# Odd layer of a two-layer backbone: one convolution beside the head projections, the normalised layer input kept in memory, and a reciprocal in four pieces

## The chip, the cores and the metric

The kernel runs on one core of a Trainium2 chip. The metric is the device time of one execution in microseconds (us), from the first to the last instruction of the core with what lies around it. TensorE is called PE in the rows, VectorE DVE, ScalarE ACT, GpSimd POOL, and SyncE SP (it only issues transfers here). A name with q behind it (SPq, ACTq) is the part of an engine that issues transfers.

## The reference, cut to what matters

The stream has 1024 latent tokens (a grid 64 wide) and 256 context tokens, 1024 wide: 10 tiles of 128 tokens, 8 latent (`LT`) and 2 context (`NT` = 10). Two layers are computed. Even layer: attention of 8 heads with 2 key heads, beside a gated product. Odd layer, at the core of this case:

```
h = rms_norm(x, norm1_g) * (1 + scale) + shift        # per stream
p = h @ w_in                                           # 1024 -> 2560 columns
q, k = per-head rms_norm of p[:, 0:512], p[:, 512:1024];  v = p[:, 1024:1536]
neighbourhood attention(q, k, v, bias tables from rpb) # latent tokens; keys also of the context
y = p[:, 1536:2048] * sigmoid(p[:, 2048:2560])         # latent tokens
y = conv(y, dw, 31 taps along the tokens, each of 512 channels by itself) + dw_b
d = silu(layer_norm(y))                                # over the 512 channels
x = x + gate * (concat(attention, d) @ w_out)
```

Each layer ends with a mixture of 16 experts (top 2 within one group of four). All arithmetic is fp32. Where the kernel can, it splits an operand into a rounded part (`hi`, type fp32r) and the rest (`lo`) and forms a product as three fast ones: hi·hi, hi·lo, lo·hi.

## The kernel before, in words

The program is a list of stages (`Phase`), each with its own buffers and semaphores, and a barrier of all engines at its end; within a stage each engine has its own list of instructions, written by hand, and waits on semaphores. `build` calls them in order: modulation, `project_even`, `attend_even`, experts and `combine` of layer 0, `project_conv` (its tiles carry the prefix pc_), `project_odd` (po_), attention of the odd layer (at_), `output_odd`, experts and `combine` of layer 1. The weights for `project_conv` (cw_w) are loaded and split during `combine`.

**The layer input.** `NormStage` makes the normalised, modulated and transposed input of one tile: load x (L277), sum of squares on ACT (L293), mean on DVE (L300), power on POOL (L307, `rstd`), scale on DVE (`scale`, L312), eight transposes on PE (L322), modulation on DVE from PSUM (`modulate`, L333, eight instructions), rounding on ACT (`round_hi`, L341), rest on POOL (`rest_lo`, L345). The product is then 24 matmuls for each 512 output columns (`product`, L354). Both `project_conv` (latent tiles) and `project_odd` (all ten) run it, so eight tiles are normalised twice.

**`project_conv`.** For each latent tile: products g and a (48 matmuls), sigmoid on ACT (L767), y on DVE (L903), four transposes of y on PE (`transpose_y`, L931), copy into yT on ACT (L769). POOL also multiplies 31 taps into diagonal matrices for two of the four channel blocks (L841), and after the tiles makes the bias rows of the attention in 16 pieces of 8 columns (L818), which it stores to memory. Then the convolution of 1024 tokens in two halves q of 512: channel blocks 0 and 1 on PE, 31 matmuls each with the diagonals (L964); blocks 2 and 3 on DVE, one instruction for each tap (`convolve`, L865; the first tap L861), two blocks in turn. Then for each half mean (PE, L953), subtraction (`centre`, DVE, L872), square (ACT, L789), variance (PE, L953), root (ACT, L783), reciprocal (L879) and multiplication (L882) on DVE, silu (ACT, L794), and a store.

**`project_odd`.** It loads and splits three 512-column parts of w_in in 16 pieces (L391, L398, L405), then for each tile: products q, k and v (72 matmuls; 48 for context tiles), squares on ACT (L1064, L1066), sums on DVE (L1127, L1129), the power -1/2 on POOL (L1099), multiplications on DVE from PSUM (L1137, L1138: `qk_done`), head gains on POOL for q (L1103) and on DVE for k (L1141), transposes (L1160, L1167), split on ACT and DVE (L1072, L1076, L1144, L1148), and stores from the ACT queue. PE starts the q product of the next tile when `qk_done` has come. SP also copies the bias rows into 96 tables, memory to memory (L1028).

**`attend_even`** runs by a planner: `EvenPlan` writes one list of events for all engines; `finish` and `prepare` give each event of a tile a due place from 0 to 19 among the tile's score steps. The event `normal` holds the reciprocal of the softmax sums (L1523, 512 columns) and the multiplication behind it (L1527); 'max' events (L1510) on DVE free the PSUM banks into which PE writes the next scores (L1599) and transposes (L1635).

Of the kernel before, what the change touches and what calls it, by code (L numbers as in the profile page):

```python
# [31 lines left out]
P = 128  # L32
D = 1024
KD = D // P
# [659 lines left out]
def project_conv(nc, k, w, dw, dw_b, ln_g, ln_b, rpbs, skews):  # L694

    CC = BW // P
    QT = 4 * P
    PC = 2  # L700
    NQ = SEQ // QT
    with Phase(nc, "pc") as ph:
        tiles = list(range(LT))
        ns = NormStage(ph, k, 1, tiles, k.stream_mid, False)
        sg, y = ph.sb("sg", [P, BW]), ph.sb("y", [P, BW])
        yT = ph.sb("yT", [P, CC, SEQ + 2 * HALO])
        acc = [ph.sb(f"acc{q}", [P, CC, QT]) for q in range(NQ)]
        diag = [ph.sb(f"diag{c}", [P, CONV, P]) for c in range(PC)]
        eps = ph.sb("eps", [P, 1])
        sq = ph.sb("sq", [P, CC, QT])  # L710
        rstd = ph.sb("rstd_c", [P, QT])
        var = ph.sb("var", [P, QT])
# [15 lines left out]
        DVE_CHUNKS = list(range(PC, CC))  # L728
        ND = len(DVE_CHUNKS)

        with nc.Block() as block:

            @block.sync
            def _(sp):
                ns.load_columns(sp)
                ns.load(sp, 0)
                ns.load(sp, 1)
                sp.wait_ge(R["zero"], 2)
                for o in range(2):
                    sp.dma_start(bias_rows[o][:, P // 2 - 16:P // 2 + 15], rpbs[o].rearrange("h r c -> (h r) c")).then_inc(R["bias_in"], 16)  # L740
                for i in range(2, LT):
                    ns.load(sp, i)
# [7 lines left out]
            def _(act):  # L750
# [2200 lines left out]
```

## Time and profile before

| what | value |
|---|---|
| median of 3 runs | 3231.34 us (3231.14 to 3236.19) |
| the profiled execution, its own time | 3228.54 us |
| its span | 3226.8 us |
| PE busy | 2489.5 us (77%) |
| DVE busy | 1559.2 us (48%) |
| ACT busy | 1006.9 us (31%) |
| POOL busy | 605.6 us (19%) |
| granted clock of PE, mean | 0.887 of full speed |

The table gives shares of the whole span. The kernel is a row of stages with different limits, so a share says little about one of them; the rows below are of the stages that the change touches. The chain that ended last reaches back only to 3164 us, within the last stage, so it doesn't help here.

### The profile page before, as it was taken

The page shows a single profiled execution, that of the slowest core. Times are in us where ns is not written, and L with a number is a line of the kernel's source. Part 1 is how long each engine was busy: PE and PEld are TensorE (multiplying, and loading weights), DVE is VectorE, ACT ScalarE, POOL GpSimd, SP SyncE. Part 2 cuts the span into 40 slices and gives each one's busy share as a digit, 9 for nine tenths or more (in the row PEclk, how much of TensorE's full clock was granted, in tenths as well). Part 3 has the DMA queues.
Part 4 walks back from the last instruction along what each step waited for, and adds up shares of the span by engine and source line. Part 5 has one row for each costly group of instructions (what it writes and reads, how often), then busy time and mean ns, then how long its engine had stood idle before and what let it go on. Part 6 is the DMA issues. An engine that isn't in the chain of part 4 may idle for free. (4 is left out here: it accounts for less than half of the span.)

```text
span 3226.8 us, 31983 instructions
## 1 busy us (share of the span) xinstructions
PE 2489.5 (77%) x10785; PEld 1803.0 (56%) x10786; DVE 1559.2 (48%) x2144; ACT 1006.9 (31%) x1326; POOL 605.6 (19%) x560
## 2 busy tenths in 40 slices
PE   5499788898943999999217778498699773999990
PEld 0388655565622888887005533376465662888770
DVE  2255553443333566555442494333477225566754
ACT  1122143233312455444001101222265112455640
POOL 0233212111112000000122340133131332000002
PEclk9999899998966999999558889699899885999995
DMA  9210236111046767663860140665683325778846
GB/s 388 64 50 36 89 131 221 42 47 59 30 178 164 290 253 272 228 248 118 340 234 27 55 135 13 164 154 135 182 214 87 125 90 200 270 271 307 322 176 221
DMA packets 304557, 534.58 MB, mean 166 GB/s; under 512 B 126157, under 2 KB 150203, under 8 KB 298300
## 3 DMA queue, kind: packets, MB, share of 16 engines
q1 hardware_dynamic: 228848, 387.56, 35.9%
q0 software_dynamic: 25520, 85.58, 7.7%
q10 hardware_dynamic: 50076, 59.99, 5.4%
q8 instruction: 64, 1.05, 0.1%
q14 instruction: 49, 0.40, 0.0%
HBM read 431.72 MB, written 116.03 MB: 170 GB/s over the span
## 5 line engine op out<-in xcount | busy, mean ns | idle before, releaser
L2597 DVE TENSOR_TENSOR ex_gu_lo<-mw_gu,ex_gu_hi 128x2048 fp32r<-128x2048 f32 x128 | 287.4, 2288 | 77.8 <-ACT ex_gu_hi L2517 77.5
L2517 ACT ACTIVATE ex_gu_hi<-mw_gu 128x2048 fp32r<-128x2048 f32 x128 | 237.5, 1910 | 122.9 <-DVE ex_y L2644 117.6
L1627 PE MATMUL at_ps_o<-at_pT,at_v_one 128*128 128x512 f32 x336 | 177.6, 610 | 12.5 <-ACT at_total L1409 9.4
L2675 PE MATMUL ex_ps_g<-ex_gu_hi,ex_xT_hi 128*128 128x512 f32 x408 | 169.1, 414 | 8.7 <-issue 5.3
L2675 PE MATMUL ex_ps_y<-ex_d_hi,ex_hT_hi 128*128 128x512 f32 x408 | 166.5, 408 | 9.1 <-DVE ex_d_lo L2597 7.7
L2597 DVE TENSOR_TENSOR ex_d_lo<-mw_d,ex_d_hi 128x2048 fp32r<-128x2048 f32 x64 | 143.8, 2288 | 53.3 <-ACT ex_d_hi L2517 53.3
L2492 POOL TENSOR_TENSOR ex_at<-ex_slots,ex_nil 128x1 int32<-128x1 int32 x53 | 17.7, 333 | 801.2 <-PE ex_ps_x L2669 796.6
L2675 PE MATMUL ex_ps_g<-ex_gu_lo,ex_xT_hi 128*128 128x512 f32 x408 | 164.1, 402 | 0.0
L2675 PE MATMUL ex_ps_g<-ex_gu_hi,ex_xT_lo 128*128 128x512 f32 x408 | 164.0, 402 | 0.0
L1399 ACT ACTIVATE at_pT<-at_ps_s 128x512 f32<-128x512 f32 x168 | 99.0, 595 | 204.6 <-PE at_ps_s L1620 204.2
L2675 PE MATMUL ex_ps_y<-ex_d_lo,ex_hT_hi 128*128 128x512 f32 x408 | 161.7, 396 | 0.0
L2675 PE MATMUL ex_ps_y<-ex_d_hi,ex_hT_lo 128*128 128x512 f32 x408 | 161.7, 396 | 0.0
L2675 PE MATMUL ex_ps_u<-ex_gu_hi,ex_xT_hi 128*128 128x512 f32 x408 | 161.2, 395 | 0.0
L2675 PE MATMUL ex_ps_u<-ex_gu_lo,ex_xT_hi 128*128 128x512 f32 x408 | 161.2, 395 | 0.0
L2675 PE MATMUL ex_ps_u<-ex_gu_hi,ex_xT_lo 128*128 128x512 f32 x408 | 161.1, 395 | 0.0
L2517 ACT ACTIVATE ex_d_hi<-mw_d 128x2048 fp32r<-128x2048 f32 x64 | 119.1, 1909 | 29.4 <-DVE ex_y L2619 20.7
L1510 DVE TENSOR_REDUCE at_mx<-at_ps_t 128x1 f32<-128x512 f32 (+1 forms) x168 | 108.6, 683 | 25.6 <-PE at_ps_t L1599 25.1
L2006 PE MATMUL at_ps_o<-at_pT,at_vo 128*128 128x512 f32 (+3 forms) x256 | 113.2, 523 | 1.2 <-ACT at_pT L1829 0.8
L865 DVE SCALAR_TENSOR_TENSOR pc_acc<-pc_yT,pc_taps,pc_acc 128x512 f32<-128x512 f32 x120 | 112.9, 1017 | 0.0
L964 PE MATMUL pc_ps_c<-pc_yT,pc_diag 128*128 128x512 f32 x248 | 109.9, 604 | 1.6 <-ACT pc_acc L776 1.6
L1599 PE MATMUL at_ps_t<-k_both,at_q_both 128*128 128x512 f32 (+1 forms) x208 | 99.4, 546 | 14.7 <-DVE at_mx L1510 10.9
L2517 ACT ACTIVATE ex_xT_hi<-ex_ps_x 128x512 fp32r<-128x512 f32 x106 | 57.8, 596 | 169.2 <-PE ex_ps_x L2669 169.2
(492 smaller groups left out, 5907.1 us busy)
## 6 DMA issues: line engine op xcount, KB each, us to landing
mw_gu<-in_moe_w_gate SPq DMA_DIRECT2D x32, 2048.0 KB, 10.7
mw_gu<-in_moe_w_up SPq DMA_DIRECT2D x32, 2048.0 KB, 15.7
mw_d<-in_moe_w_down SPq DMA_DIRECT2D x32, 2048.0 KB
y_d<-ex_y ACTq DMA_DIRECT2D x51, 512.0 KB
mod_mod_w<-in_ada_w SPq DMA_DIRECT2D x24, 1024.0 KB, 10.9
y_d<-at_zero POOLq DMA_DIRECT2D x36, 512.0 KB, 5.1
co_mod_w<-in_ada_w SPq DMA_DIRECT2D x16, 1024.0 KB, 13.8
edge_d<-rows_d SPq DMA_DIRECT2D x64, 160.0 KB, 3.4
```

The source lines that it names most:

```text
L865: ins = nc.vector.scalar_tensor_tensor(acc[q][:, c, :], src, taps[:, c, t:t + 1], acc[q][:, c, :], ALU.mult, ALU.add)
L964: mm = nc.tensor.matmul(ps_c[:, :], diag[c][:, t, :], yT[:, c, q * QT + t:q * QT + t + QT], start=(t == 0), stop=(t == CONV - 1))
L1399: nc.scalar.activation(pT[u % 3][:, :], ps_s[u % 3][:, :], ACT.Exp).then_inc(S["exp_done"], 1)
L1510: nc.vector.tensor_reduce(mx[:, heads[0]:heads[-1] + 1, c], src.rearrange("p (h t) -> p h t", t=size), AX.X, ALU.max).then_inc(read, 1)
L1599: mm = nc.tensor.matmul(flat[:, n * size:(n + 1) * size], q_both[i % 2][g][:, j * P:(j + 1) * P], k.k0_both[:, g, a:a + size], start=True, ...
L1627: nc.tensor.matmul(ps_o[:, :], v_one[:, kt, g:g + 2, :].rearrange("p a d -> p (a d)"), pT[u % 3][:, :], start=(u == plan.first[i, g]), sto ...
L2006: nc.tensor.matmul(ps_o[g][:, c0 * P:c1 * P], vo[h % 2][:, kt, :, :].rearrange("p a d -> p (a d)"), pT[s % 3][:, 0:n], start=(s == plan.fi ...
L2492: nc.gpsimd.tensor_tensor(at[:, :], slots[:, bass.ds(within(n, most), 1)], nil[:, :], ALU.add).then_inc(S["at_ready"], 1)
L2517: nc.scalar.activation(dst, src, ACT.Copy).then_inc(sem, 1)
L2597: sub = lambda dst, a, b, sem: nc.vector.tensor_tensor(dst, a, as_f32(b), ALU.subtract).then_inc(sem, 1)
L2675: mm = nc.tensor.matmul(out, a[:, c, :], b[:, c, cols], start=(c == 0 and j == 0), stop=(c == chunks - 1 and j == 2))
```

## The change

It does three things.

1. `project_conv` and `project_odd` are replaced by `project_tiles` and `project_heads`, with `OddShared` holding what both need. `project_tiles` normalises all ten tiles once and stores the hi and lo parts of each to a new memory tensor hT_d; makes a, g and y of the latent tiles as before; loads and splits the q and k weights between the tiles (two pieces of 512 columns each tile); makes the bias rows between the tiles, in 32 pieces of 4 columns; and starts the first 48 table copies from tile 5 on. No convolution is in it.
2. `project_heads` loads the hi and lo parts from memory instead of normalising, splits the v weights on ACT and POOL, and computes the heads as before with single instead of double output buffers and the stores moved to SP. The convolution of all four channel blocks runs on DVE between the head instructions: 124 instructions, each over all 1024 tokens of a block. Mean, variance and what follows them stand among the two context tiles. The diagonal matrices and their matmuls are gone.
3. In `attend_even` the reciprocal is cut in four of 128 columns, at due places 1, 1, 2 and 3, and what follows it is due one place later.

Core of the diff:

```diff
@@ project_tiles
-        tiles = list(range(LT))
-        ns = NormStage(ph, k, 1, tiles, k.stream_mid, False)
+        tiles = list(range(NT))
+        ns = NormStage(ph, k, 1, tiles, k.stream_mid, True)
...
-                ns.load_columns(sp)
                 ns.load(sp, 0)
                 ns.load(sp, 1)
+                ns.load_columns(sp)
...
+                for i in range(NT):
+                    if i + 2 < NT:
+                        ns.load(sp, i + 2)
+                    sp.wait_ge(ns.lo_done, i + 1)
+                    for n, src in enumerate((ns.hi, ns.lo)):
+                        sp.dma_start(k.hT_d[i, n], as_f32(src[i % 2][:, :, :])).then_inc(h_out[i % 2], 16)
+                    if i + 1 < LT:
+                        o.w_qk.load(sp, 2 * i + 2, 2 * i + 4)
...
+                    if i >= 5:
+                        o.copy_tables(sp, k, 0, 10 * (i - 5), 10 * (i - 4))
...
                     if i < LT:
+                        o.w_qk.round_hi(act, 2 * i, 2 * i + 2)
+                    if 0 < i <= LT:
                         j = i - 1
                         act.wait_ge(S["gemm_g"], i)
...
+                    if i == 0:
+                        pool.wait_ge(R["bias_in"], 32)
+                    if i < LT:
+                        for n in range(NP * i // 4, NP * (i + 1) // 4):
+                            mask_rows(n)
...
+                    if i < LT:
+                        o.w_qk.rest_lo(dve, 2 * i, 2 * i + 2)
@@ project_heads
+        wv_hi, wv_lo, wv_raw = w.hi[:, :, 0:BW], w.lo[:, :, 0:BW], w.raw
...
+        acc = ph.alias("acc", w.lo, [P, KD, 2 * BW])[:, :, BW:2 * BW]
...
+                for c in range(KD):
+                    pool.wait_ge(S["wv_hi"], c + 1)
+                    nc.gpsimd.tensor_tensor(wv_lo[:, c, :], wv_raw[c % 2][:, :], as_f32(wv_hi[:, c, :]), ALU.subtract).then_inc(S["wv_lo"], 1)
...
+                def convolve(n):
+
+                    for t, c in steps[done[0]:done[0] + n]:
+                        src = o.yT[:, c, t:t + SEQ].rearrange("p (q t) -> p q t", q=NQ)
...
+                            dve.wait_ge(S["conv_done"], done[0] - CC + 1)
+                            ins = nc.vector.scalar_tensor_tensor(both(c), src, o.taps[:, c, t:t + 1], both(c), ALU.mult, ALU.add)
...
                 dve.wait_ge(S["gains_in"], 32)
...
+                convolve(8)
+                for j in range(NT):
...
+                    convolve(5)
...
+                    nc.vector.tensor_reduce(stat[:, h0:], per_head(sq[:, c0:]), AX.X, ALU.add).then_inc(S["sums_done"], 1)
...
+                    convolve(4)
...
+                    convolve(6)
+                    dve.wait_ge(S["kT_hi"], j + 1)
...
+                    product(ps_k[:, :], j, o.w_qk.hi, o.w_qk.lo, BW).then_inc(S["gemm_k"], 1)
+                    if j == LT:
+                        mean(0)
+                        mean(1)
+                    if j == LT + 1:
+                        variance(0)
@@ EvenPlan.finish
-        return [(1, ('normal', i)), (3, ('mixed', i)), (5, ('out', i, 0)), (8, ('out', i, 1)), (11, ('square', i)), (12, ('mean', i)),
...
+        return [(1, ('invert', i, 0)), (1, ('invert', i, 1)), (2, ('invert', i, 2)), (3, ('invert', i, 3)), (3, ('normal', i)),
+                (4, ('mixed', i)), (6, ('out', i, 0)), (9, ('out', i, 1)), (12, ('square', i)), (13, ('mean', i)),
```

Names as in the rows: cv_ is what `OddShared` holds (yT, taps, the q and k weights), po_acc the sum of the convolution.

VectorE, one latent tile of the head stage. Before (with the normalisation of the next tile in it):

```order
L333 TENSOR_SCALAR po_hf<-po_pt,po_cols 128x128 x8
L300 TENSOR_SCALAR po_ms<-po_ss 128x1
L312 TENSOR_SCALAR po_x<-po_x,po_rstd 128x1024
L1127 TENSOR_REDUCE po_stat<-po_sq 128x16
L1129 TENSOR_SCALAR po_stat<-po_stat 128x16
L1137 TENSOR_TENSOR po_qk<-po_ps_q,po_r 128x512
L1138 TENSOR_TENSOR po_qk<-po_ps_k,po_r 128x512
L1141 TENSOR_TENSOR po_qk<-po_qk,po_gains 128x512
L1144 TENSOR_TENSOR po_k_lo<-po_ps_kT,po_k_hi 128x512
L1148 SCALAR_TENSOR_TENSOR po_q_lo<-po_ps_qT,po_q_hi 128x512
```

and now:

```order
L1076 SCALAR_TENSOR_TENSOR po_acc<-cv_yT,cv_taps,po_acc 128x2x512 x5
L1102 TENSOR_REDUCE po_stat<-po_sq 128x16
L1104 TENSOR_SCALAR po_stat<-po_stat 128x16
L1076 SCALAR_TENSOR_TENSOR po_acc<-cv_yT,cv_taps,po_acc 128x2x512 x4
L1117 TENSOR_TENSOR po_qk<-po_ps_q,po_r 128x512
L1118 TENSOR_TENSOR po_qk<-po_ps_k,po_r 128x512
L1120 TENSOR_TENSOR po_qk<-po_qk,po_gains 128x512
L1076 SCALAR_TENSOR_TENSOR po_acc<-cv_yT,cv_taps,po_acc 128x2x512 x6
L1128 TENSOR_TENSOR po_k_lo<-po_ps_kT,po_k_hi 128x512
L1132 SCALAR_TENSOR_TENSOR po_q_lo<-po_ps_qT,po_q_hi 128x512
```

The ten instructions of the normalisation have left the stage; 15 of the convolution stand in their place, nine of them ahead of `qk_done` (L1118).

VectorE in `attend_even`, where the sums of one tile are inverted while the maxima of the next are taken. Before:

```order
L1501 SCALAR_TENSOR_TENSOR at_q_rest<-at_ps_t,at_q_both 64x512 x2
L1523 RECIPROCAL at_sums<-at_sums 128x512
L1527 TENSOR_TENSOR at_aT<-at_total,at_sums 128x512
L1510 TENSOR_REDUCE at_mx<-at_ps_t 128x1 x3
L1531 TENSOR_TENSOR at_aT_lo<-at_ps_t,at_aT_hi 128x512
```

and now:

```order
L1508 SCALAR_TENSOR_TENSOR at_q_rest<-at_ps_t,at_q_both 64x512 x2
L1531 RECIPROCAL at_sums<-at_sums 128x128 x2
L1517 TENSOR_REDUCE at_mx<-at_ps_t 128x1 x2
L1531 RECIPROCAL at_sums<-at_sums 128x128
L1517 TENSOR_REDUCE at_mx<-at_ps_t 128x1
L1531 RECIPROCAL at_sums<-at_sums 128x128
L1536 TENSOR_TENSOR at_aT<-at_total,at_sums 128x512
```

The first maxima stand behind two short reciprocals instead of a long one and the multiplication.

## Rows read from the trace of the kernel before

**Rows 1.** Windows: stretch, length, busy us (count) of PE, PEld, DVE, ACT, POOL, clock, DMA, GB/s.

```profile
1663.00:1851.00 188.00, 119.18 (x484) 96.42 (x485) 59.49 (x104) 25.65 (x40) 52.82 (x38) 0.79 0.17 45
1851.00:2022.00 171.00, 129.11 (x282) 55.03 (x280) 114.58 (x117) 19.53 (x21) 43.11 (x34) 0.88 0.28 81
2022.00:2080.00 58.00, 27.02 (x80) 19.20 (x80) 19.96 (x31) 16.52 (x21) 3.42 (x3) 0.66 0.54 143
2080.00:2287.00 207.00, 168.35 (x745) 135.16 (x745) 72.66 (x154) 42.44 (x71) 66.43 (x35) 0.92 0.57 146
```

**Rows 2.** Timeline, tiles of project_conv: start us, us, instruction, idle before it and releaser.

```profile
1689.98 7.30 DVE L312 TENSOR_SCALAR pc_x<-pc_x,pc_rstd 128x1024 f32<-128x1024 f32 x1 [1.74 <-POOL pc_rstd L307]
...
1747.29 0.60 ACT L769 ACTIVATE pc_yT<-pc_ps_yT 128x512 f32<-128x512 f32 x1 [17.16 <-PE pc_ps_yT L931]
1751.80 0.75 DVE L312 TENSOR_SCALAR pc_x<-pc_x,pc_rstd 128x1024 f32<-128x1024 f32 x1 [0.72 <-POOL pc_rstd L307]
1752.60 1.97 PE L322 MATMUL pc_pt<-ident,pc_x 128*128 128x128 f32 x8 [5.35 <-DVE pc_x L312]
1767.63 0.60 ACT L769 ACTIVATE pc_yT<-pc_ps_yT 128x512 f32<-128x512 f32 x1 [17.28 <-PE pc_ps_yT L931]
```

**Rows 3.** Timeline of the convolution on VectorE, with and without GpSimd at work.

```profile
1904.26 4.82 DVE L865 SCALAR_TENSOR_TENSOR pc_acc<-pc_yT,pc_taps,pc_acc 128x512 f32<-128x512 f32 x4
1905.63 2.90 POOL L818 TENSOR_TENSOR pc_rows<-pc_skew,pc_bias_rows 120x1024 f32<-120x1024 f32 x1 [1.01 <-DMA pc_skew<-in_k_skew]
...
1943.36 2.29 DVE L882 TENSOR_TENSOR pc_acc<-pc_acc,pc_rstd_c 128x2048 f32<-128x2048 f32 x1
1945.57 21.29 DVE L865 SCALAR_TENSOR_TENSOR pc_acc<-pc_yT,pc_taps,pc_acc 128x512 f32<-128x512 f32 x32
```

**Rows 4.** Groups by line in project_conv: busy us, mean ns, idle before.

```profile
L964 PE MATMUL pc_ps_c<-pc_yT,pc_diag 128*128 128x512 f32 x248 | 109.9, 604 | 1.6 <-ACT pc_acc L776 1.6
L818 POOL TENSOR_TENSOR pc_rows<-pc_skew,pc_bias_rows 120x1024 f32<-120x1024 f32 x16 | 41.5, 2594 | 14.3 <-DMA pc_skew<-in_k_skew 14.3
L953 PE MATMUL pc_ps_mu<-pc_acc,pc_mean_w 128*128 128x512 f32 x16 | 7.3, 601 | 1.7 <-DVE pc_acc L865 0.9 <-issue 0.8
```

**Rows 5.** Timeline of one latent tile of project_odd.

```profile
2102.98 0.47 PE L354 MATMUL po_ps_k<-po_w_hi,po_hi 128*128 128x512 f32 x1
2108.68 0.39 PE L354 MATMUL po_ps_v<-po_w_hi,po_hi 128*128 128x512 f32 x1
2111.20 1.21 DVE L1127 TENSOR_REDUCE po_stat<-po_sq 128x16 f32<-128x1024 f32 x1
2112.70 2.91 POOL L1099 TENSOR_TENSOR po_r<-po_stat,mhalf 128x16 f32<-128x16 f32 x1 [2.20 <-DVE po_stat L1129]
2115.65 0.69 DVE L1137 TENSOR_TENSOR po_qk<-po_ps_q,po_r 128x512 f32<-128x512 f32 x1 [3.02 <-POOL po_r L1099]
2117.01 1.79 POOL L1103 TENSOR_TENSOR po_qk<-po_qk,po_gains 128x512 f32<-128x512 f32 x1 [1.40 <-DVE po_qk L1138]
```

**Rows 6.** SP queue in project_odd: the 16 weight pieces.

```profile
2028.07 47.27 SPq L391 DMA_DIRECT2D po_w_raw<-in_od_w_in x16
```

**Rows 7.** Timeline: the last root of project_conv, and the next stage's first instruction.

```profile
2007.75 0.69 ACT L783 ACTIVATE pc_var<-pc_ps_var,pc_eps 128x512 f32<-128x512 f32 x1 [4.19 <-PE pc_ps_var L953]
...
2022.80 2.37 SPq L269 DMA_DIRECT2D po_cols<-mod_d  x4
```

**Rows 8.** The tile edge_d, written by the larger table copies.

```profile
DMA to landing us min/median/max: 2.9/3.6/15.0
```

**Rows 9.** Waits of TensorE in even attention: us in total, times, longest.

```profile
PE at_ps_t L1599 <- DVE at_mx L1510: 10.9, 9, 2.6
PE at_ps_t L1635 <- DVE at_mx L1510: 9.5, 3, 4.1
```

**Rows 10.** The tile at_sums: reciprocals of both sizes, ns min/median/max.

```profile
L1947 DVE RECIPROCAL at_sums<-at_sums x32: 894/940/953, 2351.6 to 2498.8; 128x128 f32<-128x128 f32 x32
L1523 DVE RECIPROCAL at_sums<-at_sums x10: 3333/3334/3353, 452.1 to 896.8; 128x512 f32<-128x512 f32 x10
```

More of the change, by code:

```diff
@@ L1030, in _ @@
[L1030 to L1034 removed]
+                for j in range(NT):
+                    if j + 2 < NT:
+                        load(j + 2)
+                    o.copy_tables(sp, k, 1, 5 * j, 5 * j + 5)
+                    store(j)
+                for q in range(NQ):
+                    sp.wait_ge(S["silu_done"], CC * (q + 1))
+                    sp.dma_start(k.mT_d.rearrange("(c p) t -> p c t", p=P)[:, :, q * QT:(q + 1) * QT], part(q)).then_inc(S["stored"], 16)
@@ L1080, in _, with square, root @@
-                store_heads(NT - 1)
-                for p in range(2):
-                    act.wait_ge(head_out[p], stored(NT - 2 + p))
+                def square(q):
+                    act.wait_ge(S["centred"], q + 1)
+                    if q:
+                        act.wait_ge(S["var_full"], q)
+                    nc.scalar.activation(csq[:, :, :], part(q), ACT.Square).then_inc(S["squared"], 1)
+                def root(q):
+                    act.wait_ge(S["var_full"], q + 1)
+                    nc.scalar.activation(var[:, q, :], var_bank[q][:, 0:QT], ACT.Sqrt, bias=eps[:, 0:1]).then_inc(S["var_ready"], 1)
@@ L1151, in _, with product @@
             @block.tensor
             def _(pe):
-                ns.transposes(pe, 0)
-                def transpose_k(j):
+                def product(out, j, w_hi, w_lo, a, by_chunk=False):
+                    hi, lo = h_hi[j % 2], h_lo[j % 2]
+                    for c in range(KD):
+                        if by_chunk:
+                            pe.wait_ge(S["wv_lo"], c + 1)
+                        for n, (x, y) in enumerate(((hi, w_hi), (hi, w_lo), (lo, w_hi))):
+                            mm = nc.tensor.matmul(out, x[:, c, :], y[:, c, a:a + BW], start=(c == 0 and n == 0), stop=(c == KD - 1 and n == 2))
+                    return mm
@@ L1168, in transpose_k, with mean, variance @@
                         mm.then_inc(S["qT_full"], 1)
+                def mean(q):
+                    pe.wait_ge(S["conv_done"], CONV * CC)
+                    for c in range(CC):
+                        mm = nc.tensor.matmul(mu_bank[q][:, :], mean_w[:, :], acc[:, 2 * c + q, :], start=(c == 0), stop=(c == CC - 1))
+                    mm.then_inc(S["mu_full"], 1)
+                def variance(q):
+                    pe.wait_ge(S["squared"], q + 1)
+                    for c in range(CC):
+                        mm = nc.tensor.matmul(var_bank[q][:, 0:QT], mean_w[:, :], csq[:, c, :], start=(c == 0), stop=(c == CC - 1))
+                    mm.then_inc(S["var_full"], 1)
@@ L1191 @@
+                    product(ps_v[:, :], j, wv_hi, wv_lo, 0, by_chunk=(j == 0)).then_inc(S["gemm_v"], 1)
+                    if j == LT + 1:
+                        variance(1)
+                turn(NT - 1)
 class EvenPlan:
```

544 lines of the change are left out of this document (234 added, 310 removed).

## The prediction

> **What bounds the kernel now.** I read the odd projection first as windows [rows 1]. `project_conv` and `project_odd` take 188 + 171 + 58 + 207 = 624 us of the span of 3226.8. In the first window TensorE is busy 119 of 188 us and VectorE 59: neither is full, so what bounds it is a chain through the engines. The timeline of its tiles [rows 2] shows that chain: the copies of yT stand 1767.63 - 1747.29 = 20.3 us apart, and in each tile TensorE idles 5.35 us until the scaled x comes. The second window is the convolution: 110 us of it are the matmuls with the diagonals [rows 4], and VectorE has 115 busy us beside them, so that the two halves of the work end about together. The third window is 58 us of loading and splitting 16 weight pieces, 47.3 us from first to last issue [rows 6], with TensorE 27 us busy. The fourth is nine tiles in 207 us, TensorE 168 us busy: near its own bound. So the 110 us of convolution on TensorE lie on the path, while VectorE idles 207 - 73 = 134 us in the fourth window. The question is how much VectorE can take there, and what else shares its time.
>
> **VectorE's price for the convolution.** Alone, 32 steps of 512 elements took 21.29 us, 0.665 each; an instruction of 2048 elements took 2.21 us to the start of the next (1945.57 - 1943.36) [rows 3]. A step of 1024 costs between half of 2.21, 1.11, and 0.665 + 512 x (2.21 - 0.665)/1536 = 1.18. I take 1.14, since four blocks in turn leave two more instructions between dependent steps than two did. 124 steps are 141 us.
>
> GpSimd adds to it. In [rows 3] four steps took 4.82 us instead of 4 x 0.665 = 2.66: 2.1 us were lost to one GpSimd instruction of 2.9. In the new head stage GpSimd has two instructions in each tile: the power, 2.91 us with VectorE idle, and the gains of q, 1.79 us, of which some 0.6 were a wait for VectorE's own gains that began together with it, so 1.2 [rows 5]. The power is the unknown: it handles 16 columns only, and no VectorE instruction ran beside it before. Its cost to VectorE lies between 0 and 2.9 us a tile. I take 2.9, since the nearest row, the 2.9 us instruction of [rows 3], held the steps almost whole.
>
> The Trainium skill (SBUF — State Buffer, Who interferes with whom) speaks against this change here: a VectorE instruction with two inputs in SBUF and a GpSimd one that reads SBUF exclude each other for the whole instruction. The trace agrees for the bias rows (2.1 lost of 2.9); for the power no row shows it. By the rule the power costs 2.9 a tile; without it the stage would be 23 us shorter.
>
> **The pace of a head tile.** VectorE does for one latent tile 15 steps (17.1), the sum and its scaling (1.4), two multiplications, the k gains and two splits of 0.6 to 0.7 each (3.3), together 21.8, plus 2.9 and 1.2 for GpSimd, and 0.4 for ScalarE's rounding of q: 26.3 us. TensorE needs three products of 5.7 (2108.68 - 2102.98 [rows 5]), and 1 for transposes, 18 us, 21 with the half clock that it shows after an idle time (eight transposes in 1.97 us at 1752.60 behind 5.35 us idle, granted clock 0.79 in that window) [rows 1, 2]. So VectorE becomes the bound of the latent tiles and TensorE idles 5 to 8 us in each; its slower clock is hidden under VectorE. The normalisation of x is gone from this stage.
>
> **The head stage, summed.** Start: eight v weight pieces, at 47.27/16 = 2.95 us each 24 us; VectorE waits for the gains, which SP issues behind them, although its first steps need no gain. Then 13 steps (4 of them first taps), sum, 4 steps, power, multiplications: 24 us. First `qk_done` at 48. Seven more tiles at 26.3: 232. Then, with the convolution done, the two context tiles carry its normalisation, and the chain is TensorE's again: transposes and the k product at half clock in part 11, two means 7.3 (3.65 each [rows 4]), product v 5.7, product k 5.7, variance 3.7, product v 5.7, variance 3.7, together 43; from the root to the end 15.0 as before (2022.80 - 2007.75 [rows 7]), and 3 for handovers: 61. Stage: 293 us, barrier included.
>
> **The tile stage.** Removed: the diagonals. The second scale took 7.30 us instead of 0.75 because of one [rows 2], and it stands on the path: -6.5; x is now loaded ahead of the columns and weights: -3. Added to the cycle of 20.3: two weight roundings of 0.6 ahead of the sigmoid, of which 0.7 are covered by the wait of the scale for GpSimd (idle 0.72 [rows 2]); and the first bias-row piece, half of 2.59 [rows 4], starts just as the scale is released and delays it by 0.8. Pace 21.6; seven times +1.3 is +9. GpSimd itself has 2.9 for the tile and four pieces at 2.7 to 4 (half of 2.59, two issues, and the load of the next piece): 14 to 19 of 21.6 us, just hidden. One more set of transposes ahead of the last product: +2. So the latent tiles end at 188 + 1 = 189 us. Behind them: transposes, modulation, rounding and rest of the last context tile, 8 (5 to 12), then its store, queued behind ten table copies (landing of such a copy 3.6 us median, 15.0 at most [rows 8]): 12, and 3 for landing and barrier. Stage: 212 us.
>
> The split of the q and k weights, 16 pieces, moves into the tiles and is hidden in VectorE's and ScalarE's idle time (60 and 26 busy of 188 [rows 1]). The mean 0.28 to 0.57 of the DMA engines leaves room for the stores and loads of hT_d.
>
> New: 212 + 293 = 505, plus 2 for the barrier between; before 624. **Change: -117 us.**
>
> **The even reciprocal.** TensorE waits 10.9 + 9.5 = 20.4 us for VectorE's maxima [rows 9], almost all of it where the reciprocal of 3.33 us stands ahead of them. Four pieces take 4 x 0.94 = 3.76 [rows 10], but two maxima now stand behind 1.9 us instead of 3.33 + 0.69. Bounds: all 20.4 gone, or none and 10 x 0.43 = 4 us lost. I take -13, two thirds, since the waits for a bank shrink but don't end.
>
> **Sum.** -117 - 13 = -130 us. The profiled execution took 3228.5, so 3098.5; the median of the runs is 2.8 above it: 3101. I forecast 3100 us.
>
> **Rivals.**
>
> 1. The power doesn't hold VectorE. For it: 16 columns, no row. Then a latent tile is 23.4 us, near TensorE's own 21, and the time 3100 - 23 = 3077.
> 2. SP's queue becomes the bound in the tile stage's end. 18 table copies, the last stores and then the first loads of the head stage stand in one queue. For it: 15.0 us to land at worst [rows 8]. If each copy takes 2 us more than I assume, the last store and the first load come 35 us later: 3135. Against it: the median of 3.6 at a DMA share of 0.57.
> 3. It gets slower. VectorE's steps of two rows of 512 in a shared buffer cost as much beside GpSimd as the old ones did: 4.82/4 = 1.2 us for 512 elements [rows 3], 2.4 for 1024. Place: the latent tiles of the head stage. Price: 124 x (2.4 - 1.14) = 156 us, to 3256. It decides from 1.14 + 130/124 = 2.2 us a step. Against it: GpSimd was busy 41.5 us with bias rows [rows 4] beside the steps of before, and will be 4 in 26.
> 4. The change doesn't do what it says: the aliasing of hT and weights forces TensorE to wait for loads, so that nothing overlaps. The order shows each load two tiles ahead, and I give it no chance of its own.
>
> **How the numbers follow.** My case 0.62, rival 1 0.18, rival 2 0.15, rival 3 0.03, something outside 0.02. Runs of this kernel differ by 0.16%, so 0.2% (6.5 us) is about what can be told from no change. All cases but the third lie 80 us or more below: faster 0.96, same 0.01, slower 0.03. The range takes in rival 1 with the full even gain (3077 - 7, and 10 for a head pace set too high) and rival 2 with no even gain (3135 + 13): 3060 to 3150.
>
> **What would show it.** Right: the first stage near 212 us with copies of yT 21 to 22 us apart; a head stage of about 293 with `qk_done` 26 us apart, VectorE over 90% busy in it and TensorE idle 5 us or more a tile for L1118; steps of 1.14 us; TensorE's waits for the maxima in even attention [rows 9] under 10 us in all. Step by step wrong: steps of a mean beyond 1.6 us (rival 3); a pace under 24 (rival 1); first instruction of the head stage to first `qk_done` over 60 us, or yT copies over 24 apart (rival 2, or GpSimd's bias rows on the path).

## The result, and the profile after

The changed kernel took 3075.82 us (median of 4, 3068.45 to 3077.09), the kernel before 3232.40 beside it: a ratio of 0.9513, 95% interval 0.9502 to 0.9525. Forecast were 3100, between 3060 and 3150. The profiled execution has a span of 3073.8 us, 153.0 less than before. The two forecast gains came out far from their sizes, in opposite directions:

| stretch | before | forecast | after |
|---|---|---|---|
| even attention | 552.9 | -13 | 552.5 |
| odd projection: stage of the tiles | | 212 | 195.6 |
| odd projection: stage of the heads | | 293 | 272.8 |
| odd projection in all | 623.5 | -117 | 468.4, -155.1 |
| from there to the end | 939.7 | 0 | 943.0 |

The last row lies within its own spread: in the eleven experiments below that keep all work the same stretch took 939 to 944 us, and the change doesn't touch it.

The windows of the odd projection after, with the columns of [rows 1]: stage of the tiles; heads, up to the first `qk_done`; from there to the last latent one; the rest.

```profile
1662.00:1858.00 196.00, 118.21 (x500) 96.17 (x500) 67.42 (x127) 38.63 (x63) 104.38 (x121) 0.78 0.75 220
1858.00:1904.00 46.00, 19.66 (x72) 15.10 (x72) 20.81 (x20) 6.62 (x11) 14.20 (x11) 0.69 0.52 136
1904.00:2072.00 168.00, 139.86 (x560) 112.44 (x560) 164.01 (x155) 19.41 (x35) 39.54 (x14) 0.86 0.45 122
2072.00:2131.00 59.00, 39.62 (x144) 27.28 (x144) 27.39 (x23) 18.07 (x22) 5.04 (x3) 0.82 0.45 131
```

In the third VectorE (third of the busy times) is busy 164 of 168 us. The 110 us of matmuls of [rows 4] are gone, and VectorE's steps fill the time in which it idled before. A latent tile on VectorE and GpSimd, from the timeline:

```profile
1946.99 0.17 DVE L1104 TENSOR_SCALAR po_stat<-po_stat 128x16 f32<-128x16 f32 x1
1947.07 4.87 DVE L1076 SCALAR_TENSOR_TENSOR po_acc<-cv_yT,cv_taps,po_acc 128x1024 f32<-128x1024 f32 x4
1951.86 0.68 DVE L1117 TENSOR_TENSOR po_qk<-po_ps_q,po_r 128x512 f32<-128x512 f32 x1
1952.46 0.68 DVE L1118 TENSOR_TENSOR po_qk<-po_ps_k,po_r 128x512 f32<-128x512 f32 x1
1953.17 0.69 DVE L1120 TENSOR_TENSOR po_qk<-po_qk,po_gains 128x512 f32<-128x512 f32 x1
1953.78 8.29 DVE L1076 SCALAR_TENSOR_TENSOR po_acc<-cv_yT,cv_taps,po_acc 128x1024 f32<-128x1024 f32 x6
1962.56 0.69 DVE L1128 TENSOR_TENSOR po_k_lo<-po_ps_kT,po_k_hi 128x512 fp32r<-128x512 f32 x1 [0.49 <-ACT po_k_hi L1038]
...
1947.24 3.86 POOL L1057 TENSOR_TENSOR po_r<-po_stat,mhalf 128x16 f32<-128x16 f32 x1 [16.34 <-DVE po_stat L1104]
1953.22 1.79 POOL L1060 TENSOR_TENSOR po_qk<-po_qk,po_gains 128x512 f32<-128x512 f32 x1 [2.11 <-DVE po_qk L1118]
```

Four steps beside the power take 4.87 us: 1.20 each, the length that steps have here without GpSimd too (6.06 for five). The power held nothing; it grew itself, from 2.91 [rows 5] to 3.86. The six steps beside the multiplication by the gains took 8.29 where 6 x 1.20 give 7.27 with the end of the last: 1.0 lost. In the whole the tiles stand 24.0 us apart, forecast 26.3. Of the 24.0, some 0.5 is the wait for the rounded k (last row of VectorE above), which comes through TensorE's q product. In the profile of experiment 10, whose edit doesn't touch this stage, that product took 7.2 us up to the transposes in place of 7.9, since TensorE left the half clock earlier; VectorE waited for nothing in four tiles there, and these stood 23.4 us apart. One of them, up to the rest of k, which has no idle time before it:

```profile
1952.53 0.47 PE L1146 MATMUL po_ps_q<-cv_w_qk_hi,cw_w_hi 128*128 128x512 f32 x1 [4.32 <-DVE po_qk L1120]
...
1959.69 0.60 PE L1154 MATMUL po_ps_kT<-ident,po_qk 128*128 128x128 f32 x4
...
1961.24 0.68 DVE L1130 TENSOR_TENSOR po_k_lo<-po_ps_kT,po_k_hi 128x512 fp32r<-128x512 f32 x1
```

So TensorE's slower clock is not quite hidden under VectorE.

The tile stage, one tile (before: [rows 2]):

```profile
1757.05 0.15 DVE L300 TENSOR_SCALAR pc_ms<-pc_ss 128x1 f32<-128x1 f32 x1 [11.73 <-ACT pc_junk L293]
1758.57 0.69 DVE L862 TENSOR_TENSOR pc_y<-pc_ps_a,pc_sg 128x512 f32<-128x512 f32 x1 [1.37 <-ACT pc_sg L799]
1759.18 1.53 DVE L312 TENSOR_SCALAR pc_x<-pc_x,pc_rstd 128x1024 f32<-128x1024 f32 x1
1760.77 1.97 PE L322 MATMUL pc_pt<-ident,pc_x 128*128 128x128 f32 x8 [6.37 <-DVE pc_x L312]
...
1763.39 0.63 PE L354 MATMUL pc_ps_g<-cw_w_hi,pc_lo 128*128 128x512 f32 x1
1763.82 0.46 PE L354 MATMUL pc_ps_g<-cw_w_hi,pc_hi 128*128 128x512 f32 x1
1764.12 0.39 PE L354 MATMUL pc_ps_g<-cw_w_lo,pc_hi 128*128 128x512 f32 x1
```

Both delays that were forecast are here: y waits for the sigmoid behind the weight rounding, and the scale takes 1.53 us in place of 0.75, since a bias-row piece runs beside it. TensorE's idle time is 6.37 in place of 5.35. Yet the pace is 20.5 us, against 20.3: behind the longer idle time TensorE left the half clock earlier (experiment 10 has the other case).

TensorE's waits in even attention (total, times, longest), after; those for the maxima are now L1608 alone:

```profile
PE at_ps_t L1608 <- DVE at_mx L1517: 8.7, 11, 1.7
PE at_ps_t L1663 <- POOL at_h L1477: 7.9, 1, 7.9
PE at_ps_t L1616 <- DVE at_nmx L1526: 7.4, 4, 2.8
PE at_ps_g L1587 <- DVE at_aT_lo L1540: 7.2, 2, 7.1
PE at_ps_t L1608 <- DVE at_aT_lo L1540: 5.4, 4, 1.4
```

The 20.4 us of [rows 9] fell to 8.7, under the 10 that were forecast, and the stage gained 0.4.

### The profile page after: what moved, and what is told of

It is laid out like the page before. It is cut to its first block and busy times, and to the rows that moved or that the text cites. A ratio compares the mean times of both kernels' runs of the same rounds, so it can differ in the third digit from the quotient of the medians.

```text
span 3073.8 us, 31336 instructions
## 1 busy us (share of the span) xinstructions
PE 2371.0 (77%) x10473; PEld 1751.4 (57%) x10474; DVE 1573.2 (51%) x2093; ACT 984.7 (32%) x1304; POOL 601.2 (20%) x598
## 5 line engine op out<-in xcount | busy, mean ns | idle before, releaser
L1076 DVE SCALAR_TENSOR_TENSOR po_acc<-cv_yT,cv_taps,po_acc 128x1024 f32<-128x1024 f32 x120 | 153.6, 1344 | 0.0
L1608 PE MATMUL at_ps_t<-k_both,at_q_both 128*128 128x512 f32 (+1 forms) x208 | 103.1, 561 | 17.5 <-DVE at_mx L1517 8.7
L1144 PE MATMUL po_ps_q<-cv_w_qk_hi,cw_w_hi 128*128 128x512 f32 x128 | 56.1, 517 | 64.7 <-DVE po_qk L1118 44.1
```

Source lines behind the costliest of these rows:

```text
L1076: ins = nc.vector.scalar_tensor_tensor(both(c), src, o.taps[:, c, t:t + 1], both(c), ALU.mult, ALU.add)
L1144: mm = nc.tensor.matmul(out, x[:, c, :], y[:, c, a:a + BW], start=(c == 0 and n == 0), stop=(c == KD - 1 and n == 2))
L1608: mm = nc.tensor.matmul(flat[:, n * size:(n + 1) * size], q_both[i % 2][g][:, j * P:(j + 1) * P], k.k0_both[:, g, a:a + size], start=True, ...
```

## The experiments

Each is an edit of the changed kernel; where only a stage is read, one execution was profiled.

**1. Even attention as before** (one reciprocal, earlier due times) inside the changed kernel.

```
-        return [(1, ('invert', i, 0)), ... (2, ('invert', i, 2)), (3, ('invert', i, 3)), (3, ('normal', i)), (4, ('mixed', i)), ...
+        return [(1, ('invert', i, 0)), (1, ('normal', i)), (3, ('mixed', i)), ...
```

> The new kernel with even attention exactly as before: one reciprocal of 3.33 us a tile, every later piece of a tile's end due one slot earlier. Theory A (the 17 us of waits for the maxima that the four pieces removed came back as waits for aT and as half-clock time of TensorE): even attention takes 552.9 us here as in the kernel before, TensorE's waits for the maxima are 20 us again, and the whole kernel is 0 to 1 us slower than the new one. Rival B (the four pieces do gain what was forecast, and something at the start of the stage hid it in the one profile): the stage takes 560 us or more, the kernel 8 to 13 us longer than the new one.

Measured: 3081.70 us (ratio 0.9541, 0.9525 to 0.9557), the stage 553.5, and TensorE's waits for the maxima 10.0 + 9.8 us. The stage and the waits are A's. The whole is 5.9 us longer than the changed kernel (9 by the ratios), between A's 0 to 1 and B's 8 to 13; in the profile 5.4 of it stand between even attention and the tile stage (735.0 us in place of 729.6), which the edit doesn't touch. So the whole decides nothing here.

**2. Four pieces at the old due times.**

```
+        return [(1, ('invert', i, 0)), (1, ('invert', i, 1)), (1, ('invert', i, 2)), (1, ('invert', i, 3)), (1, ('normal', i)), (3, ('mixed', i)), ...
```

> The new kernel with the reciprocal in four pieces, but all pieces due in slot 1 and everything behind them due where it was before the change. Theory A1 (the later due times gave the gain back): the stage takes 540 to 546 us, 7 to 12 less than in either kernel, and TensorE's waits behind aT_lo (5.4 us) are gone. Theory A2 (four pieces with nothing between them cost what one did, and TensorE's clock sets the rest): 552 us, within 2 us of both kernels, with TensorE's busy time and waits adding up as before.

Measured: 3077.43 us (0.9528, 0.9512 to 0.9543), the stage 556.5, and nearly the waits of the kernel before. A1's 540 to 546 falls, and A2's 552 within 2 is missed by some 3. The waits of its TensorE:

```profile
PE at_ps_t L1608 <- DVE at_mx L1517: 10.0, 10, 1.7
PE at_ps_t L1644 <- DVE at_mx L1517: 9.6, 3, 4.1
```

**3. One reciprocal at the new due times.**

```
-                        c = slice(ev[2] * P, (ev[2] + 1) * P)
-                        nc.vector.reciprocal(sums[:, c], sums[:, c]).then_inc(S["summed"], 1)
+                        nc.vector.reciprocal(sums[:, :], sums[:, :]).then_inc(S["summed"], 1)
```

> The new kernel with one reciprocal of 3.33 us again, but the new, later due times. The even stage took 549.8 to 553.6 us in seven profiles of the new form, 552.9 and 553.5 in the old, 556.5 with four pieces at the old due times. Theory A (the due times help and the four pieces cost a little, 3.7 us of work for 3.33): 548 to 552 us, no more than the new form. Rival B (the pieces are what helps, the later due times cost): 555 or more.

Measured: 3081.23 us in one run, the stage 555.9, as B has it: the later due times cost where the reciprocal is whole. But in experiment 2 the pieces without them cost too, so neither helps alone. With the ten profiles in which even attention is as changed (549.8 to 553.6 us, mean 551.9), the four forms are:

| | old due times | new due times |
|---|---|---|
| one reciprocal | 552.9, 553.5 | 555.9 |
| four pieces | 556.5 | 551.9 |

The cells but the last are one profile each, or two. Each part alone read some 3 us slower, both together 1.3 faster. Since the same form differs by 3.8 from run to run, only the size is shown: the edit is worth between nothing and 3 us, not 13. Theory A of experiment 1, that the waits came back elsewhere, fits the rows of the two kernels. Of the shares they show this: the maxima gave 11.7 us and TensorE's wait "issue" at them 5.4; waits for aT_lo took back 5.4, for the shifts 2.7 (7.4, 4.7 before), for the loads of q 4.4 (23.7, 19.3 before), and TensorE's busy time grew by 4.6 for the same 1890 matmuls:

```profile
380.60:933.50 552.90, 466.98 (x1890) 309.03 (x1890) 225.50 (x328) 188.41 (x328) 88.01 (x89) 0.93 0.27 92
```

(before), and after:

```profile
380.20:932.70 552.50, 471.59 (x1890) 310.52 (x1890) 225.87 (x358) 187.39 (x328) 88.13 (x89) 0.92 0.28 92
```

**4. More work for GpSimd's power.**

```
+                        n = 16 if j < 4 else 64
+                        nc.gpsimd.tensor_tensor(extra[:, 1, 0:n], extra[:, 0, 0:n], bc(k.mhalf[:, 0], 1, n), ALU.pow)
```

> GpSimd raises constants to the power -0.5 once more in each latent tile of the head stage, behind the gains of q and beside VectorE's steps; its result is used by nothing. 16 columns in tiles 0 to 3, 64 in tiles 4 to 7. Theory A (GpSimd's power does not hold VectorE: four steps beside it took 4.87 us, 1.20 each, and the power itself grew from 2.91 to 3.87): the pace stays at 24.1 us in both halves, and steps keep their 1.20. Rival B (the power holds VectorE for its length, as forecast): 27 us a tile in the first half and 30 or more in the second. Between them, a hold only while the columns are read and written: under 0.5 us for 16 columns, up to 1 for 64.

Measured: pace 23.9 in both halves, head stage 272.6 us. The power of 64 columns ran for 11.5 us, and six steps beside it (and beside the gains, as before) took 8.32 in place of 8.28:

```profile
2029.43 8.32 DVE L1081 SCALAR_TENSOR_TENSOR po_acc<-cv_yT,cv_taps,po_acc 128x1024 f32<-128x1024 f32 x6
...
2028.87 1.78 POOL L1063 TENSOR_TENSOR po_qk<-po_qk,po_gains 128x512 f32<-128x512 f32 x1 [2.11 <-DVE po_qk L1123]
2030.62 11.49 POOL L1066 TENSOR_TENSOR po_extra<-po_extra,mhalf 128x64 f32<-128x64 f32 x1
```

Theory A holds: the time that GpSimd's power runs costs VectorE nothing. What did hold VectorE in these traces were GpSimd's instructions over 512 columns and more; whether it is their size or their kind that decides, no run separates.

**5. The head stage without its taps.** Only the four first taps are computed.

```
-                steps = [(t, c) for t in range(CONV) for c in range(CC)]
+                steps = [(0, c) for c in range(CC)]
```

> Leaves out the convolution's taps 1 to 30: only the four first taps are computed, all other instructions stay. Theory A (VectorE is the bound of the latent tiles, TensorE waits 44 us in all for the multiplied k): the pace falls from 24.1 to 19 to 20.5 us, TensorE's own, with TensorE idle under 2 us a tile; the head stage takes 272.8 - 7 x 4.3 - 15 (13 steps at its start) = 228 us. Rival B (what bounds a tile is a chain through all engines, of which the steps are only a part): pace 21.5 or more, and TensorE still idle over 3 us a tile.

Measured: pace 18.63 us, head stage 224.7, TensorE idle 1.10 us a tile at a granted clock of 1.00 (0.86 with the steps). Theory A holds (the pace is a little under its 19), and TensorE's own tile is 18.6. The whole took 3063.56, and everything behind the head stage 978 us in place of 943: the stages behind work on other data there, which may be why, so that only the head stage is compared.

**6. The gains of q on VectorE.**

```
-                        nc.gpsimd.tensor_tensor(per_head(qk[:, 0:BW]), per_head(qk[:, 0:BW]), bc(gains[:, 0, :], 1, H), ALU.mult
+                        nc.vector.tensor_tensor(per_head(qk[:, 0:BW]), per_head(qk[:, 0:BW]), bc(gains[:, 0, :], 1, H), ALU.mult
```

> The gains of q are multiplied in on VectorE, behind those of k, and GpSimd keeps only the power. Theory A (GpSimd's multiplication holds VectorE for 1.0 us: six steps took 8.28 us where others at 1.20 give 7.27; on VectorE it takes 0.6): pace 24.0 - 0.4 = 23.5 to 23.6, head stage 3 us shorter, and six steps behind it take 7.3. Rival B (the 8.28 are something else, such as TensorE's or ScalarE's traffic): pace 24.5, stage 4 to 5 us longer.

Measured: pace 23.96, stage 272.8: no gain, where A had 23.5 to 23.6. The six steps did come down, to 7.26:

```profile
2000.01 0.68 DVE L1114 TENSOR_TENSOR po_qk<-po_ps_k,po_r 128x512 f32<-128x512 f32 x1
2000.72 0.69 DVE L1116 TENSOR_TENSOR po_qk<-po_qk,po_gains 128x512 f32<-128x512 f32 x1
2001.34 0.68 DVE L1119 TENSOR_TENSOR po_qk<-po_qk,po_gains 128x512 f32<-128x512 f32 x1
2001.94 7.26 DVE L1072 SCALAR_TENSOR_TENSOR po_acc<-cv_yT,cv_taps,po_acc 128x1024 f32<-128x1024 f32 x6
2010.07 0.69 DVE L1127 TENSOR_TENSOR po_k_lo<-po_ps_kT,po_k_hi 128x512 fp32r<-128x512 f32 x1 [0.87 <-ACT po_k_hi L1038]
```

but VectorE then waits 0.87 us for the rounded k. From `qk_done` on, TensorE's q product, the transposes and ScalarE's rounding take 10.0 us; what VectorE saves in that half of a tile becomes waiting.

**7. The same, with one step moved across.**

```
-                    convolve(4)
+                    convolve(3)
...
-                    convolve(6)
+                    convolve(7)
```

> As gains_dve, with 5 + 3 + 7 steps in a latent tile in place of 5 + 4 + 6. Theory A (a tile has two halves: from qk_done to the rest of k VectorE waits for TensorE's chain, which takes 10.0 us, from there to the next qk_done it is bound by itself; what GpSimd gave back only made the wait longer, 0.87 for 0.41 us, and a step moved into the first half takes it off the second): pace 22.9 to 23.2. Rival B (the chain moves along with the steps): 24.0 as before.

Measured: pace 23.48 us, stage 268.7. A gain of 0.5 a tile where 1.0 was expected: the direction is A's, and B falls. VectorE no longer waits for the rounded k, but the three steps left in the second half are shorter than the power beside them:

```profile
2024.19 3.67 DVE L1072 SCALAR_TENSOR_TENSOR po_acc<-cv_yT,cv_taps,po_acc 128x1024 f32<-128x1024 f32 x3
2028.26 0.69 DVE L1113 TENSOR_TENSOR po_qk<-po_ps_q,po_r 128x512 f32<-128x512 f32 x1 [0.40 <-POOL po_r L1057]
```

Each half of a tile has a bound of its own. The gain is small beside what the unedited stage shows by itself: it ran at 24.0 where VectorE waited for the rounded k, and at 23.4 in four tiles of the profile of experiment 10, where it didn't. What the experiment shows is that the wait is gone in all tiles, in one profile.

**8. Twenty steps ahead of the gains.**

```
-                dve.wait_ge(S["gains_in"], 32)
-                convolve(8)
+                convolve(20)
+                dve.wait_ge(S["gains_in"], 32)
```

and 4 + 4 + 5 steps in place of 5 + 4 + 6.

> 20 convolution steps ahead of VectorE's wait for the gains (before: 8, behind it), and 4 + 4 + 5 steps in each latent tile in place of 5 + 4 + 6. Theory A (VectorE bounds the latent tiles: 24.0 us with 15 steps, 18.6 with none, where TensorE bounds): two steps less are 2.4 us less, pace 21.5 to 21.7, first qk_done 13 x 1.2 = 15.6 us earlier less what the pieces of v still take, some 13; head stage 272.8 - 7 x 2.4 - 13 = 243 us. Rival B (steps at the start collide with GpSimd's rests of the v weights, 1.27 us each, and delay them as the steps with bias rows did): first qk_done less than 6 us earlier, stage 250 or more.

Measured: 3060.45 us in one run, stage 261.7 (A had 243), pace 21.0 to 22.0 behind a first tile of 22.7, about A's 21.5 to 21.7, but the first `qk_done` at 50.2 us in place of 46.1, as B has it. What came late are the rests of the v weights. GpSimd's rows, and VectorE's beside them:

```profile
1860.21 19.22 DVE L1076 SCALAR_TENSOR_TENSOR po_acc<-cv_yT,cv_taps,po_acc 128x1024 f32<-128x1024 f32 x16
1865.04 16.75 POOL L1052 TENSOR_TENSOR cw_w_lo<-cw_w_raw,cw_w_hi 128x512 fp32r<-128x512 f32 x2 [7.53 <-ACT cw_w_hi L1016]
1883.91 1.26 POOL L1052 TENSOR_TENSOR cw_w_lo<-cw_w_raw,cw_w_hi 128x512 fp32r<-128x512 f32 x1 [2.12 <-ACT cw_w_hi L1016]
L1052 POOL TENSOR_TENSOR cw_w_lo<-cw_w_raw,cw_w_hi x8: 1261/1274/15515, 1865.0 to 1894.9; 128x512 fp32r<-128x512 f32 x8
```

Two rests of 1.26 us each took 16.75. VectorE's row of 16 steps was 19.22 us long without a gap, and lost nothing. It was the first rest that took 15.5 us: it began at 1865.04, saw eleven more steps start, and ended at 1880.55, 1.1 us behind the row. The next loads of v pieces were issued only then, at 1880.58.

**9. The last table copies in the head stage.**

```
-                    if i >= 5:
+                    if 5 <= i < 9:
...
+                o.copy_tables(sp, k, 0, 40, 48)
```

> The last eight table copies of the tile stage are issued in the head stage, behind the gains, and not behind the last stores of the tile stage. Theory A (SP issues copies for 6.6 us behind the last store, and the barrier comes 1.3 us after the last of them): the tile stage takes 195.6 - 6 = 189 to 191 us, since the store itself needs 2 to 3 us to land, and the head stage stays 272.8. Rival B (the copies hide behind the landing of the stores and of the copies issued before): under 1 us.

Measured: from the last copy of yT to the head stage 14.0 us in place of 16.5, the head stage 272.0 us. The gain is 2.5 us, between A's 5 to 7 and B's 1: SP's last store was issued at 1848.3, and 5.3 us passed until the next stage, for landing and barrier, where A took 3 to 4. The tile stage as a whole took 195.6 us, as in the changed kernel, since its first yT came 1.7 us later; in eight other profiles with the copies as before it took 195.6 to 198.5, and 194.6 and 193.7 in experiments 11 and 12, which have this edit too.

**10. No delay of the scaled x.**

```
-                    if i < LT:
-                        o.w_qk.round_hi(act, 2 * i, 2 * i + 2)
...
                         nc.scalar.activation(sg[:, :], ps_g[:, :], ACT.Sigmoid).then_inc(S["sg_done"], 1)
+                    if i < LT:
+                        o.w_qk.round_hi(act, 2 * i, 2 * i + 2)
...
                     if i < LT:
+                        pool.wait_ge(ns.xn_done, i + 2)
```

> In the tile stage ScalarE rounds the two pieces of q/k weights behind the sigmoid and not ahead of it, and GpSimd's first bias-row piece waits for VectorE's scale. Both take a delay off the scaled x (y waited 1.37 us for the sigmoid, 0.33 before; the scale took 1.53 us, 0.75 before), so TensorE's idle time goes from 6.37 back to 4.6 to 5.4 us a tile. Theory A (idle time adds to the tile): pace 20.5 - 1.0 to 1.8 = 18.7 to 19.5 us. Rival B (TensorE runs at half clock for a shorter time behind a longer idle time: 3.2 us behind 6.37, 4.8 behind 5.35, so that idle time and slow time trade against each other): pace 20.2 to 20.5.

Measured: both delays are gone, TensorE idles 5.37 us, and the pace is 19.9 to 20.5 us, mean 20.29 (20.57 as changed). A tile:

```profile
1760.34 1.97 PE L322 MATMUL pc_pt<-ident,pc_x 128*128 128x128 f32 x8 [5.37 <-DVE pc_x L312]
...
1764.67 0.63 PE L354 MATMUL pc_ps_g<-cw_w_hi,pc_hi 128*128 128x512 f32 x1
1765.09 0.47 PE L354 MATMUL pc_ps_g<-cw_w_lo,pc_hi 128*128 128x512 f32 x1
1765.40 0.39 PE L354 MATMUL pc_ps_g<-cw_w_hi,pc_lo 128*128 128x512 f32 x1
```

B holds for the pace. 1.0 us less idle time bought 0.3 (0.8 in the first tile, 0.04 in the last), since the half clock then lasted to 4.75 us behind the restart (1765.09 - 1760.34), with 6.37 idle only to 3.05. It is so in all tiles: 3.9 to 4.8 us with 5.37 us of idle time, 2.6 to 3.5 with 6.37, and in the kernel before, with 5.35, 4.3 to 4.8. The stage as a whole was not shorter, 197.1 us: its first yT came at 53.7 us, in the changed kernel at 50.7.

**11. What these point to, together:** the rests of v on VectorE, two steps behind each (20 steps ahead of the gains); 4 + 3 + 6 steps; the copies of experiment 9. Its core:

```
+                convolve(4)
+                for c in range(KD):
+                    dve.wait_ge(S["wv_hi"], c + 1)
+                    nc.vector.tensor_tensor(wv_lo[:, c, :], wv_raw[c % 2][:, :], as_f32(wv_hi[:, c, :]), ALU.subtract).then_inc(S["wv_lo"], 1)
+                    convolve(2)
                 dve.wait_ge(S["gains_in"], 32)
-                convolve(8)
```

> As steps_early, with the eight rests of the v weights on VectorE, each followed by two steps (20 steps in all ahead of the gains), 4 + 3 + 6 steps in a latent tile, and the last table copies in the head stage. Theory A (in steps_early a run of 16 steps kept GpSimd's two rests waiting, 16.75 us for 2.52 us of work, and with them the loads of the v pieces; where VectorE does the rests itself nothing waits): the pieces keep their 3 us, first qk_done 33 to 38 us into the stage in place of 46.1, pace 20.3 to 21.2, head stage 240 to 247 us, tile stage and copies 2 to 3 us less; whole kernel 3045 to 3052 us, 25 to 30 below the new one. Rival B (the late rests were the loads' own lateness): first qk_done at 50 us again, whole kernel 3060 or more.

Measured: 3053.34 us (median of 5, 3049.35 to 3063.30), ratio 0.9449, 0.9431 to 0.9467: faster than the changed kernel too, but just outside A's 3045 to 3052. The pieces keep their 3 us, as A says, and B's late pieces are ruled out. The first `qk_done` came at 42.9 us and the pace at 21.5 to 22.2, both above what was expected: I had counted too little of the first tile's own 4 + 3 steps into the start, and VectorE waits 0.4 us a tile for the power behind three steps and up to 0.6 for the rounded k. Head stage 253.5 us, expected 240 to 247.

**12. The rests back on GpSimd, with a wait of VectorE for each.** The edit is against experiment 11.

```
-                    dve.wait_ge(S["wv_hi"], c + 1)
-                    nc.vector.tensor_tensor(wv_lo[:, c, :], wv_raw[c % 2][:, :], as_f32(wv_hi[:, c, :]), ALU.subtract).then_inc(S["wv_lo"], 1)
+                    dve.wait_ge(S["wv_lo"], c + 1)
```

> As best, with the eight rests of the v weights back on GpSimd; VectorE waits for each of them before the two steps that follow it, so that it leaves a gap for every rest. Theory A (GpSimd gets at memory only where VectorE's row of steps has a gap; 16 steps without one held a rest for some 15 us): each rest takes 1.3 us, up to 3.7 where two steps are still running, the pieces come 3 to 4 us apart, first qk_done 43 to 48 us into the stage (best: 42.9), pace 21.7 as in best, whole kernel within 6 us of best. Rival B (what delayed the rests was the number of steps ahead, not the missing gap): single rests of 5 us and more, first qk_done 50 us or later.

Measured: 3057.21 us, 0.9457 (0.9441 to 0.9473); first `qk_done` at 46.2, pace 21.5 to 21.9, and no rest longer than 2.29 us:

```profile
L1053 POOL TENSOR_TENSOR cw_w_lo<-cw_w_raw,cw_w_hi x8: 1268/1678/2289, 1863.5 to 1882.3; 128x512 fp32r<-128x512 f32 x8
```

A's numbers came true: with the same number of early steps the longest rest went from 15.5 us to 2.3, so the number of steps (B) is not what delayed it. A's reason, that GpSimd gets in only at a gap, is not borne out by the same profile. VectorE waited with idle time for two rests alone, the first (5.84 us) and the third (1.18), and the last five rests (one from 1871.75 on, the others from 1875.24, 1876.57, 1879.88 and 1882.30) ran beside a row of VectorE that has no gap:

```profile
1871.82 24.39 DVE L1077 SCALAR_TENSOR_TENSOR po_acc<-cv_yT,cv_taps,po_acc 128x1024 f32<-128x1024 f32 x16 [1.18 <-POOL cw_w_lo L1053]
1875.24 3.52 POOL L1053 TENSOR_TENSOR cw_w_lo<-cw_w_raw,cw_w_hi 128x512 fp32r<-128x512 f32 x2 [2.19 <-ACT cw_w_hi L1017]
1879.88 4.49 POOL L1053 TENSOR_TENSOR cw_w_lo<-cw_w_raw,cw_w_hi 128x512 fp32r<-128x512 f32 x2 [1.11 <-ACT cw_w_hi L1017]
```

Each got in behind at most one step, and the step beside it took 2.3 us in place of 1.28: the 16 steps lost 5.2 us. The kernel before shows the same ([rows 3]): its steps of 512 columns stood in a row without a gap too, and GpSimd's bias rows took 2.4 to 2.9 us each beside them. Why one rest was let in only behind twelve steps in experiment 8, and the others behind one, stays open.

## Why the prediction was right, and where not

**The total** was within the range and 25 us too high: the odd projection was sized 38 us too dear, the even reciprocal 12.5 too good. That the two errors partly cancel is luck, and so is it that 3075.8 lies on rival 1's 3077: rival 1 has 23 us from the power alone, while the head stage came out 20 lower, the tile stage 16 lower and even attention 12.5 higher.

**What bounds the stages** was right. The convolution's matmuls lay on the path and are gone; VectorE is the bound of the latent tiles, 164 of 168 us busy, and taking its steps away (experiment 5) takes 5.4 us off each. "Its slower clock is hidden under VectorE" was so but for some 0.5 us a tile, the wait for the rounded k. TensorE idles 4.0 us a tile, a little under the 5 to 8 that were forecast, and its own 18 us were 18.6.

**The power** was the step that failed in the head pace: "I take 2.9, since the nearest row ... held the steps almost whole." It costs VectorE nothing (the timeline and experiment 4). This was the mechanism of rival 1, and -2.9 a tile is its price. The steps gave 0.9 of it back: they cost 1.20 where I had taken 1.14, just outside my ends of 1.11 and 1.18; the other terms came out 0.3 less, so that the pace is 24.0 and not rival 1's 23.4. Over the stage: seven tiles at 24.0 for 26.3 are 16 us, the first `qk_done` came at 46.1 for 48, the tail took 58.7 for 61. The nearest row was of another kind: there GpSimd's instruction read and wrote 1024 columns, the power handles 16 and computes.

The Trainium skill (SBUF — State Buffer, Who interferes with whom) has a VectorE instruction with two inputs in SBUF and a GpSimd one that reads SBUF exclude each other for the whole instruction. For GpSimd's sums, subtractions and multiplications the trace agrees: 1.0 us lost beside the gains of q, 1.0 by a step beside each rest in experiment 12. For the power it does not: 11.5 us of it cost VectorE 0.04. And one instruction's exclusion doesn't give the 15.5 us of experiment 8, in which a rest stood behind twelve steps.

**The tile stage** was 16 us too dear. The pace was taken as 20.3 + 1.3: the delays were sized rightly (0.8 and some 0.5), and their sum stands in the 6.37 us of idle time, but I added them to the pace. TensorE's clock came back earlier and repaid most of it (experiment 10), so that seven tiles took some 7 us less than forecast. Another 7 are the last context tile and its store: 15.9 us from the last copy of yT to the barrier in place of 23. The rest is the start: the first yT came at 50.7 us in place of 63.5 before, 12.8 us earlier where 9.5 were forecast. Rival 2, a late queue, did not come: the copies behind the last stores cost 2.5 us (experiment 9).

**The even reciprocal** was the worst term: -13 for some -1. "Two maxima now stand behind 1.9 us instead of 3.33 + 0.69" was right, and the waits for them went from 20.4 to 8.7. The failed step is "two thirds" of a wait taken as a gain: the aT that stands behind the reciprocal came later (four pieces with maxima between them took from 660.18 to 665.32 where one had taken 3.34), TensorE waited there instead (5.4 us at the scores for aT_lo, none before), and its 1890 matmuls took 4.6 us more at a mean clock of 0.92 in place of 0.93. Which of these follows from which is not shown. I also read the diff as a split alone and costed the moved due times at nothing, though each of the two alone reads slower (experiments 2 and 3).

**Rival 3** stayed away: GpSimd's bias rows are in the tile stage, and the steps kept 1.20 us. Its mechanism is real where GpSimd has work beside the steps, but its price is one hold for each GpSimd instruction (2.3 us for a step in place of 1.28, experiment 12) and not a dearer step throughout; and in experiment 8 it was GpSimd that waited.

## What to carry to other kernels

A wait that an edit removes is not yet time gained: follow the chain to what is late next, and look at the clock of the engine that waited. Where work is moved onto an engine that shares its way to memory, look at both: beside a long row of one engine an instruction of the other took twelve times its own length here, and with a wait for each of them in the row it didn't. A tile with two halves has two bounds; spread the movable work so that both are full.

## What the runs showed of the hardware

- A GpSimd subtraction of 128x512 took 1.26 us alone and, once, 15.5 us beside a row of VectorE steps of 1024 without a gap. In experiment 12 five of them ran beside such a row in 1.3 to 2.3 us, and five steps took 2.3 us in place of 1.28. What decides between the two isn't shown.
- GpSimd's power took 2.89 us for 16 columns with VectorE idle and 3.87 beside VectorE's steps, 11.5 for 64 columns, and slowed VectorE by 0.04 us.
- In the tile stage TensorE's half clock lasted to 4.75 us behind the restart after 5.37 us of idle time, and to 3.05 us after 6.37. With 1.10 us of idle time a tile its granted clock stayed at 1.00.
- A VectorE step over 1024 elements took 1.20 us in a row of them, one over 512 0.665.
